# The first block's attention: the value products of two query tiles in one group, 256 columns wide

## The chip, the cores and the metric

The kernel runs on one core of one Trainium2 chip. The metric is the device time of one execution in microseconds (us). The kernel before took 1542.6 us, the median of 3 runs (1541.73 to 1544.58). In names of engines, PE is TensorE, ACT ScalarE, DVE VectorE, POOL GpSimd and SP SyncE.

## The reference, cut to what matters

Two blocks, each of two layers, work on 256 tokens of width 1024. The change is in the attention of the first block. Its layer 0 also updates a stream of 256 context tokens, its layer 1 does not.

```python
def first_block(...):
    for l in range(DEPTH):                       # DEPTH = 2
        ...
        o = jnp.concatenate([
            global_attention(qa, ka, va, kac, vac),            # 6 heads, 256 + 256 keys
            fourier_mix(fb),
            window_attention(qc, kc, vc, kcc, vcc, sink[l]),   # 6 heads, 256 + 256 keys, window and sink
        ], axis=-1)
        x = x + gt1 * (o @ w_out[l])
        ...
        if update_ctx:                           # layer 0 only
            oc = jnp.concatenate([
                dense_attention(qac, kac, vac),                # 6 heads, 256 keys
                fourier_mix(fbc),
                dense_attention(qcc, kcc, vcc, sink[l]),
            ], axis=-1)
            ...
```

Each attention is softmax(q k^T / 8) times v, for heads of 64 channels. Everything is in 32-bit floats.

## The kernel before, in words

Five engines run one program each, tied by semaphores that count finished work. The order on each engine is written out by hand in loops; nothing reorders it later.

**Steps and pairs.** `pairs_first` makes a list of attention steps. One step is one pair of heads and one tile of 128 queries (`u["n"]` is 0 or 1). Steps 2p and 2p+1 are the two query tiles of the same two heads: pair p. Layer 0 has 12 steps of the x stream against 512 keys (w = 512) and then 12 of the context stream against 256 keys (w = 256). Layer 1 has only the 12 of w = 512. From the seventh step of each stream on, a head has a sink, and in the x stream a window mask.

**One step** goes through these operations:

- `logits` (L1097, PE): scores of both heads into two PSUM banks.
- `shifts` (DVE): the mask is added (L2209), the row maximum taken (L2210) and turned into a shift (L2212, or L2215 and L2217 with a sink).
- `probs` (L1537, ACT): the exponential, with its row sum.
- `shares` (L2226 and L2230, DVE): division by the sum.
- `turn_probs` (L1117, PE): transposes of the probabilities, by 128 columns, into the two banks `TURN`; a step of w = 512 fills both, a step of w = 256 fills one.
- `keep_turned` (L1552, ACT): copies these banks to `probT` in SBUF. There are two places for `probT`, and a step uses the one of its number modulo 2, so step j overwrites what step j-2 left. That is why ACT first waits until the value products of step j-2 are done: `act.wait_ge(pv_done, u["step"] - 1)`. The next step's transposes wait in turn for these copies, since they need the banks.
- `values` (L1130, PE): the value products. For each of the w/128 chunks of keys and each of two heads, one product with 64 value channels as weights and the 128 turned query columns as moving data. The two heads write the upper and the lower 64 partitions of bank `OUT`, and the two steps of a pair its columns 0 to 127 and 128 to 255.
- `empty_out` (L1576, ACT): after the second step of a pair, bank `OUT` goes to `mixo`. `lead` (L1566, ACT) rounds it into the operand of the output projection, and POOL (L2735) keeps the rest.

**The order.** On PE, loop turn i issues `logits(i)`, `turn_probs(i-3)`, a piece of other work where `BESIDE_AT` has 2i, `values(i-4)`, and another piece where it has 2i+1. The other work is the modulation vectors (`ada_sums` L838, `ada_spread` L853 and L857, `ada_spread_ctx` L864; all use bank `BESIDE`) and the Fourier mixing (L1169, then L1174 and L1175). On ACT, turn i issues `keep_turned(i-3)`, `empty_out(i-4)`, `probs(i)`, in some turns the copies of the Fourier products (L1612, L1625), `lead(i-4)`, and in two turns of each layer the rounding of a weight unit for the output projection (`split_ahead`, L1428, 2048 columns): i = 11 and 14 in layer 0, i = 5 and 7 in layer 1. On DVE, turn i issues `shifts(i)`, a piece of the other work, `shares(i-1)` and another piece (L1905, L1908 and L1913 for the modulation vectors, L2285 for the Fourier mixing, L1887 for a weight unit's remainder).

Bank `OUT` is free for a new pair once `empty_out` of the pair before is done. The output projection (L823 to L825) follows on PE right behind the last value product.

## Time and profile before

| | us |
|---|---|
| median of 3 runs (range) | 1542.6 (1541.73 to 1544.58) |
| the profiled execution, its time | 1544.52 |
| its span | 1542.7 |
| the attention of layer 0 in it | 107.8 to 200.9 |
| the attention of layer 1 in it | 692.8 to 744.9 |

The span is what the profiler saw of one execution, from the first instruction to the last; the execution's own time is 1.8 us more. Times of the trace count from the start of the span. PE's busy time holds matmuls whose records overlap, since they are pipelined, so what a block of them costs is the distance from its first start to the next block's start. The trace has two records for each matmul of plain 32-bit floats: a program's eight stand as x16. Transposes have one each.

### The profile page before, as it was taken

How to read it: one execution, taken by the hardware profiler on the slowest of the kernel's cores; microseconds unless marked ns; L12 is line 12 of the kernel's file. 1: busy time of each engine (PE TensorE's matmuls, PEld its weight loads, DVE VectorE, ACT ScalarE, POOL GpSimd, SP SyncE). 2: the span in 40 equal slices, each digit the busy share in tenths (PEclk: the TensorE clock that was granted, in tenths of full speed). 3: DMA queues.
4: the chain of work that ended last, by engine and by line, in shares of the span. 5: the costliest groups of instructions: out<-in, count | busy, mean ns of one | idle time of the engine just before them, and what ended most of it. 6: DMA issues, size and time to landing. Idle time of an engine off the chain costs nothing.

```text
span 1542.7 us, 23297 instructions
## 1 busy us (share of the span) xinstructions
PE 1494.9 (97%) x9195; PEld 1254.5 (81%) x9195; DVE 1076.0 (70%) x1613; ACT 680.0 (44%) x1073; POOL 144.8 (9%) x151
## 2 busy tenths in 40 slices
PE   6999999999999999999999999899999999999998
PEld 3775579888888888885789999788988988898896
DVE  2748645778887886758466667688766777876566
ACT  3446725221121212538453333655555656455463
POOL 1210102000000000410100000321000111200002
PEclk9999999999999999999999999999999999999999
DMA  9526423454445633235345555645533555463342
GB/s 335 198 96 214 101 76 116 156 178 144 148 160 210 239 118 108 84 109 137 110 135 185 179 184 164 199 155 178 172 94 126 162 160 170 151 198 111 125 141 90
DMA packets 169422, 235.86 MB, mean 153 GB/s; under 512 B 9020, under 2 KB 116580, under 8 KB 169192
## 3 DMA queue, kind: packets, MB, share of 16 engines
q1 hardware_dynamic: 169320, 234.45, 46.7%
q8 instruction: 70, 1.15, 0.3%
q14 instruction: 32, 0.26, 0.1%
HBM read 233.38 MB, written 1.05 MB: 152 GB/s over the span
## 4 chain that ended last, share of the span: by engine, by line
PE 85%; DVE 7%; ACT 3%; issue 2%; POOL 1%; DMA 1%; SPq 0%; POOLq 0%; DVEq 0%; ACTq 0%
PE psum L823 24%; PE psum L825 23%; PE psum L824 23%; PE psum L1097 3%; PE psum L1130 3%; PE psum L1117 3%; DVE wl L1887 2%; PE psum L838 1%; PE psum L1025 1%; PE psum L957 1%; PE psum L1169 1%; ACT wh L1428 1%; DVE smax L2210 1%; DMA raw<-in_w_ada 1%; ACT hTh L1662 1%
## 5 line engine op out<-in xcount | busy, mean ns | idle before, releaser
L1887 DVE TENSOR_TENSOR wl<-raw,wh 128x2048 fp32r<-128x2048 f32 (+1 forms) x170 | 384.8, 2263 | 165.7 <-ACT wh L1428 99.0
L823 PE MATMUL psum<-hTh,wh 128*128 128x256 f32 (+1 forms) x1376 | 430.0, 313 | 5.1 <-DVE hTl L2010 3.5
L825 PE MATMUL psum<-hTh,wl 128*128 128x256 f32 (+1 forms) x1376 | 423.1, 307 | 0.0
L824 PE MATMUL psum<-hTl,wh 128*128 128x256 f32 (+1 forms) x1376 | 423.1, 307 | 0.0
L1777 ACT ACTIVATE wh<-raw 128x2048 fp32r<-128x2048 f32 x62 | 118.9, 1918 | 371.6 <-PE psum L825 371.6
L823 PEld LDWEIGHTS psum<-hTh,wh 128*128 128x128 f32 x1376 | 262.3, 191 | 23.5 <-issue 6.9
L824 PEld LDWEIGHTS psum<-hTl,wh 128*128 128x128 f32 x1376 | 262.4, 191 | 13.4 <-issue 0.7
L825 PEld LDWEIGHTS psum<-hTh,wl 128*128 128x128 f32 x1376 | 262.3, 191 | 12.6
L1428 ACT ACTIVATE wh<-raw 128x2048 fp32r<-128x2048 f32 (+2 forms) x108 | 202.4, 1874 | 108.7 <-PE psum L825 97.1
L823 PE MATMUL psum<-wh,hTh 128*128 128x512 f32 (+3 forms) x576 | 222.1, 386 | 9.3 <-DVE hTl L1989 4.0
L825 PE MATMUL psum<-wh,hTl 128*128 128x512 f32 (+3 forms) x576 | 218.0, 378 | 0.0
L824 PE MATMUL psum<-wl,hTh 128*128 128x512 f32 (+3 forms) x576 | 217.6, 378 | 0.0
L823 PEld LDWEIGHTS psum<-wh,hTh 128*128 128x128 f32 x576 | 109.0, 189 | 33.9 <-issue 8.7
L825 PEld LDWEIGHTS psum<-wh,hTl 128*128 128x128 f32 x576 | 109.0, 189 | 18.8
L824 PEld LDWEIGHTS psum<-wl,hTh 128*128 128x128 f32 x576 | 109.2, 190 | 17.3
L823 PE MATMUL psum<-wh,ffh 128*128 128x512 f32 x264 | 104.9, 397 | 0.1
L825 PE MATMUL psum<-wh,ffl 128*128 128x512 f32 x264 | 102.9, 390 | 0.0
L824 PE MATMUL psum<-wl,ffh 128*128 128x512 f32 x264 | 102.9, 390 | 0.0
L2210 DVE TENSOR_REDUCE smax<-psum 128x2 f32<-128x1024 f32 (+3 forms) x68 | 61.9, 910 | 54.4 <-PE psum L1097 31.5
L2366 DVE TENSOR_TENSOR scr<-psum,scr 128x512 f32<-128x512 f32 x108 | 70.5, 687 | 19.0 <-PE psum L825 18.7
L1552 ACT ACTIVATE work<-psum 128x512 f32<-128x512 f32 (+1 forms) x104 | 55.1, 565 | 41.0 <-PE psum L1117 40.9
L1537 ACT ACTIVATE work<-psum,shift 128x256 f32<-128x256 f32 (+4 forms) x118 | 64.5, 556 | 19.1 <-DVE shift L2212 16.6
(207 smaller groups left out, 1805.5 us busy)
## 6 DMA issues: line engine op xcount, KB each, us to landing
raw<-in_w_in SPq DMA_DIRECT2D x54, 1024.0 KB, 5.0
raw<-in_w_ada SPq DMA_DIRECT2D x24, 1024.0 KB, 5.2
raw<-in_w_gate SPq DMA_DIRECT2D x22, 1024.0 KB, 5.1
raw<-in_w_up SPq DMA_DIRECT2D x22, 1024.0 KB, 5.2
raw<-in_w_down SPq DMA_DIRECT2D x22, 1024.0 KB, 4.8
qkT<-in_w_ada SPq DMA_DIRECT2D x16, 1024.0 KB, 7.2
raw<-in_w_in SPq DMA_DIRECT2D x16, 768.0 KB, 4.5
vals<-in_w_ada SPq DMA_DIRECT2D x8, 1024.0 KB, 6.4
```

Source lines behind the costliest of these rows:

```text
L823: pe.matmul(o, left[0], right[0], start=first, stop=False)
L824: pe.matmul(o, left[0], right[1], start=False, stop=False)
L825: return pe.matmul(o, left[1], right[0], start=False, stop=last)
L1097: mm = pe.matmul(o[:, x, g * nk:g * nk + nk], u["q"][g][x], u["k"][g][x], start=g * nk % 512 == 0, stop=True, skip_group_check=True)
L1117: mm = pe.transpose(o[:, P * x:P * x + P], u["score"][:, f:f + P], ident[:, :])
L1428: act.activation(wh[:, w % SPLIT, 0:m], raw[:, u % RING, 0:m], ACT.Copy).then_inc(hi_ready, 1)
L1537: act.activation(u["score"][:, x * u["w"]:x * u["w"] + u["w"]], u["logits"][:, x, :], ACT.Exp, bias=shift[:, s, x:x + 1], scale=SCALE, acc ...
L1552: act.activation(flat[:, 512 * n:512 * n + m], ps[TURN[(u["turn0"] + n) % 2]][:, 0:m], ACT.Copy)\
L1777: act.activation(wh[:, w % SPLIT, :], raw[:, u % RING, :], ACT.Copy).then_inc(hi_ready, 1)
L1887: dve.tensor_tensor(wl[:, w % SPLIT, 0:m], raw[:, u % RING, 0:m], wh[:, w % SPLIT, 0:m].bitcast(F32), ALU.subtract).then_inc(lo_ready, 1)
L2210: link(dve.tensor_reduce(smax[:, s, :], u["logits"], AX.X, ALU.max))
L2366: dve.tensor_tensor(y, ps[down_bank(l, i, x)], y, ALU.add).then_inc(ysum_done, 1)
```

## The change

In the first block only, `values` does nothing in the first step of a pair. In the second step it makes the products of both query tiles: the two places of `probT` are read as one operand of 2 x 128 columns (`both`), so each product has 256 columns. There are eight of them for a pair of w = 512 and four for w = 256, where there were sixteen and eight. `pv_done` still rises by two for a pair, once at the last product of each head. For the first step of a pair, ACT's wait in `keep_turned` is raised by one: the copy into place 0 now waits for the whole pair before, whose products read it. The bank is asked for in the second step alone. Everything else is unchanged, `empty_out` among it, and the second block's attention too.

```diff
                 def values(u):
 
+                    if not second and u["n"] == 0:
+                        return
                     pe.wait_ge(probT_ready, u["turn1"])
                     at = OUT
+                    if not second:
+                        bank(at)
+                        n = u["w"] // P
+                        both = work[:, 3072:5120].rearrange("p (t c q) -> p t c q", t=2, q=P)
+                        for c_ in range(n):
+                            for x in range(2):
+                                mm = pe.matmul(ps[at][HD * x:HD * x + HD, 0:SEQ].rearrange("p (t q) -> p t q", t=2),
+                                               u["vs"][x][c_], both[:, :, n * x + c_, :], start=c_ == 0,
+                                               stop=c_ == n - 1, skip_group_check=True)
+                                if (c_, x) == (n - 1, 0):
+                                    mm.then_inc(pv_done, 1)
+                        mm.then_inc(pv_done, 1)
+                        freed[at] = (out_emptied, u["pair"] + 1)
+                        return
                     if u["n"] == 0:
                         bank(at)
...
                     u = steps[j]
                     if j >= 2:
-                        act.wait_ge(pv_done, u["step"] - 1)
+                        act.wait_ge(pv_done, u["step"] - 1 + (not second and u["n"] == 0))
```

PE in layer 0, from the value products of step 0 (the rows between the sums and spreads of the modulation vectors), before:

```order
L853 MATMUL psum<-adar,sel 128x512
L1130 MATMUL psum<-work,vals 64x128 x8
L864 MATMUL psum<-adar,sel 128x512
L1097 MATMUL psum<-qkT 128x512 x2
L1117 MATMUL psum<-ident,work 128x128 x8
L1130 MATMUL psum<-work,vals 64x128 x8
L838 MATMUL psum<-raw,csil 32x512 x8
```

and the same place in the changed kernel, where the value products are L1133:

```order
L853 MATMUL psum<-adar,sel 128x512
L864 MATMUL psum<-adar,sel 128x512
L1097 MATMUL psum<-qkT 128x512 x2
L1117 MATMUL psum<-ident,work 128x128 x8
L1133 MATMUL psum<-work,vals 64x256 x8
L838 MATMUL psum<-raw,csil 32x512 x8
```

The first block of value products is gone from between the two spreads, and the second is twice as wide.

PE at the end of layer 1's attention, from the transposes of step 8 to the output projection, before:

```order
L1117 MATMUL psum<-ident,work 128x128 x8
L1174 MATMUL psum<-four,dftC 128x256
L1175 MATMUL psum<-four,dftC 128x256
L1130 MATMUL psum<-work,vals 64x128 x8
L1117 MATMUL psum<-ident,work 128x128 x8
L1130 MATMUL psum<-work,vals 64x128 x8
L1169 MATMUL psum<-dftL,vals 128x512 x2
L1117 MATMUL psum<-ident,work 128x128 x8
L1130 MATMUL psum<-work,vals 64x128 x8
L1117 MATMUL psum<-ident,scr 128x128 x8
L1174 MATMUL psum<-four,dftC 128x256
L1175 MATMUL psum<-four,dftC 128x256
```

and in the changed kernel:

```order
L1117 MATMUL psum<-ident,work 128x128 x8
L1190 MATMUL psum<-four,dftC 128x256
L1191 MATMUL psum<-four,dftC 128x256
L1133 MATMUL psum<-work,vals 64x256 x8
L1117 MATMUL psum<-ident,work 128x128 x8
L1185 MATMUL psum<-dftL,vals 128x512 x2
L1117 MATMUL psum<-ident,work 128x128 x8
L1133 MATMUL psum<-work,vals 64x256 x8
L1117 MATMUL psum<-ident,scr 128x128 x8
L1190 MATMUL psum<-four,dftC 128x256
L1191 MATMUL psum<-four,dftC 128x256
```

The transposes of steps 9 and 11 now stand directly behind the wide products of pairs 3 and 4, or with the Fourier products alone between them; the value products of steps 8 and 10 are gone from there.

## Rows read from the trace of the kernel before

**Rows 1.** The page's part 1: busy time, share and instructions of each engine.

```profile
PE 1494.9 (97%) x9195; PEld 1254.5 (81%) x9195; DVE 1076.0 (70%) x1613; ACT 680.0 (44%) x1073; POOL 144.8 (9%) x151
```

**Rows 2.** Busy time by stretch (start:end, length, then engines, PE clock, DMA, GB/s).

```profile
107.80:200.90 93.10, 89.43 (x681) 49.44 (x680) 66.25 (x175) 64.45 (x178) 8.02 (x11) 0.98 0.50 148
692.80:744.90 52.10, 48.80 (x390) 28.06 (x389) 39.92 (x86) 39.89 (x96) 3.64 (x5) 1.00 0.41 102
```

**Rows 3.** Waits of PE in layer 0's attention: total, times, longest, us.

```profile
PE psum L1117 <- ACT work L1552: 2.1, 1, 2.1
PE psum L1169 <- DVE hTl L2285: 1.0, 1, 1.0
...
```

**Rows 4.** Waits of PE in layer 1's attention.

```profile
PE psum L1117 <- ACT work L1552: 1.8, 2, 1.5
PE psum L1169 <- DVE hTl L2285: 0.6, 1, 0.6
PE psum L1130 <- ACT work L1552: 0.4, 1, 0.4
PE psum L1097 <- ACT sunk L1541: 0.4, 1, 0.4
```

**Rows 5.** Timeline of PE, layer 0 (start, length, what, [idle before <-releaser]).

```profile
126.33 1.09 PE L1130 MATMUL psum<-work,vals 128*64 128x128 f32 x16
127.36 1.92 PE L838 MATMUL psum<-raw,csil 128*32 128x512 f32 x16
129.21 1.13 PE L1097 MATMUL psum<-qkT 64*128 64x512 f32 x4
130.27 1.09 PE L1117 MATMUL psum<-ident,scr 128*128 128x128 f32 x8
...
182.70 0.70 PE L1097 MATMUL psum<-qkT 64*128 64x256 f32 x4
183.33 0.66 PE L1117 MATMUL psum<-ident,work 128*128 128x128 f32 x4
183.92 0.66 PE L1130 MATMUL psum<-work,vals 128*64 128x128 f32 x8
184.50 0.70 PE L1097 MATMUL psum<-qkT 64*128 64x256 f32 x4
```

**Rows 6.** Timeline of layer 0 behind the value products of step 0: PE, then DVE.

```profile
123.19 1.13 PE L864 MATMUL psum<-adar,sel 128*128 128x512 f32 x2
...
122.46 0.69 DVE L1913 COPY gates<-psum 128x512 f32<-128x512 f32 x1
```

**Rows 7.** Timeline of ACT, layer 0, its turn 11.

```profile
158.39 1.91 ACT L1428 ACTIVATE wh<-raw 128x2048 fp32r<-128x2048 f32 x1 [0.69 <-DMA raw<-in_w_out]
```

**Rows 8.** Timeline of layer 1, turns 5 and 6: PE, then ACT.

```profile
714.72 1.06 PE L1117 MATMUL psum<-ident,work 128*128 128x128 f32 x8 [0.34 <-ACT work L1552]
...
708.89 1.08 ACT L1552 ACTIVATE work<-psum 128x512 f32<-128x512 f32 x2
710.26 0.38 ACT L1576 ACTIVATE mixo<-psum 128x256 f32<-128x256 f32 x1 [0.29 <-PE psum L1130]
...
713.97 1.09 ACT L1552 ACTIVATE work<-psum 128x512 f32<-128x512 f32 x2
716.35 1.12 ACT L1552 ACTIVATE work<-psum 128x512 f32<-128x512 f32 x2
...
718.62 0.69 ACT L1537 ACTIVATE scr<-psum,shift 128x512 f32<-128x512 f32 x1 [0.88 <-DVE sunk L2217]
```

**Rows 9.** Timeline of layer 1, its end: PE, then ACT.

```profile
733.91 1.09 PE L1117 MATMUL psum<-ident,work 128*128 128x128 f32 x8
...
743.87 1.09 PE L1130 MATMUL psum<-work,vals 128*64 128x128 f32 x16 [0.43 <-ACT work L1552]
744.89 0.50 PE L823 MATMUL psum<-wh,hTh 128*128 128x512 f32 x1
...
734.02 0.38 ACT L1576 ACTIVATE mixo<-psum 128x256 f32<-128x256 f32 x1 [1.19 <-PE psum L1130]
```

## The prediction

> **What bounds the kernel now.** I read the page's busy times first: PE is busy for 97% of the span [rows 1]. The change touches two stretches only, so I read those next. In both, PE keeps its full clock (0.98 and 1.00) and is busy for 89.4 of 93.1 us in layer 0's attention and 48.8 of 52.1 us in layer 1's; ACT is busy for 64.5 and 39.9 us [rows 2]. Two things follow. Time that a block of PE's work costs there is nearly always on the path. But the stretches are also the narrowest place for the other engines: DVE and ACT are at 70 to 77%, and each step is a ring PE, DVE, ACT, DVE, PE, ACT, PE. The waits show how near that ring is to binding: PE waits 3.1 us or so for others in layer 0 [rows 3] and 3.2 us in layer 1, three of the four kinds for ACT [rows 4]. So the change has to be read twice: as work on PE, and as new moments at which ACT may start.
>
> **Part 1: work on PE.** A block's cost is the distance between starts [rows 5]. A value block of w = 512 costs 127.36 - 126.33 = 1.03 us, one of w = 256 costs 184.50 - 183.92 = 0.58. The difference, 0.44 us, is four products of 128 columns, so a block has 1.025 - 2 x 0.44 = 0.15 us that doesn't depend on its length. The wide block is not in this trace. The nearest rows for "same matmuls, twice the columns" are the scores: 183.33 - 182.70 = 0.63 for 256 columns and 130.27 - 129.21 = 1.06 for 512, so 256 more columns of a two-head pair cost 0.43 us, in full proportion. Four such pairs and the fixed 0.15 make 1.855 us for a wide block, 1.0 for the context stream's. Bounds: 1.71 if only the columns count (four times 0.43) and nothing is fixed, and 2.05 if nothing is saved against two blocks. I take 1.855. Saved per pair: 2 x 1.025 - 1.855 = 0.20 and 2 x 0.585 - 1.0 = 0.17 us. In layer 0 that is 6 x 0.20 + 6 x 0.17 = 2.2 us, in layer 1 6 x 0.20 = 1.2 us.
>
> The Trainium skill, in "TensorE: Matmul & The Clock Gate", section "Back-to-back issue gap", gives 81 ns per matmul at 128 columns and 131 ns at 512 in a sustained stream; an estimate on a straight line between them is 98 ns at 256, so 1.57 us for the sixteen records of a wide block, 1.7 with the fixed part. The trace's sixteen records of 128 columns take 64 ns each and its scores grow in proportion, so I don't follow it. By it the sum below would be 2.2 us smaller.
>
> **Part 2: what was hidden behind the first steps' blocks.** Several removed blocks stood where PE would have waited anyway. In layer 0, the block of step 0 lies between the two spreads, and the second spread can't start before DVE has copied bank `BESIDE` (122.46 + 0.69 = 123.15; the spread starts at 123.19) [rows 6]. Without the block PE idles for 1.03 us there: nothing is gained, and the pair's work comes later on top.
>
> **Part 3: the new wait on ACT.** The first copy of every pair but the first now starts when the wide block of the pair before has ended. PE issues that block in the same turn, behind the transposes: where ACT could copy step j's transposes while PE made the products of step j-1, it now stands still for 1.86 us, plus any piece between. Behind this wait on ACT are the copies (two, 0.97 us apart from start to next start), `empty_out`, the exponentials (1.4 us), `lead` and the rounding of a weight unit (1.8 us). For ACT wait, in turn: the next step's transposes (they need both banks), the scores two steps on (exponentials free their banks), and DVE.
>
> I walked both stretches with these durations, PE, ACT and DVE side by side, each operation starting at the later of its predecessor's end and its inputs plus 0.04 us. With the order of before, the walk gives the last value block's start at 744.4 us (743.87 in the trace, [rows 9]), so it may be used for differences.
>
> *Layer 1, against before:*
>
> - Turn 5. Step 0's block is gone (-1.02), pair 0's is wide (+0.83): it ends at 710.0. ACT's copy of step 2 moves from 708.89 to 710.1 [rows 8]. ACT had 0.29 us of slack in front of `empty_out` [rows 8] and loses the rest: +0.77 on everything behind it, the rounding included. PE's transposes of step 4, which waited for ACT at 714.72 already [rows 8], come 0.77 late, whatever PE saved.
> - Turn 7. Pair 1's wide block adds 0.83, so PE is 1.6 late at its end. The copy of step 4 stands at 718.5 instead of 716.35 [rows 8]; 0.88 us of idle time before the exponentials [rows 8] takes up some of it. ACT is +1.1, with the second rounding behind it, and so are the transposes of step 6.
> - Turns 9 to 11. Pair 2 adds 0.83 (+1.9), step 6's block gives back 1.02 (+0.9), pair 3 adds 0.83 (+1.7). The transposes of step 9 come directly behind it [rows 9]; the copy of step 8 can start only then, and its first half takes 0.6: PE waits 0.7 (+2.5). ACT's exponentials of step 11 are late by as much, with them the Fourier copies: +2.7 at the next Fourier product, though step 8's block is gone.
> - The end. Pair 4 adds 0.83 and the transposes of step 11 wait 0.7 for the copy of step 10 (+4.3); step 10's block is gone, but the last block waits for its copies anyway, 1.6 us where it waited 0.43 [rows 9]; it is 0.83 longer. Layer 1: **+5.1 us**, which is -1.2 of work and +6.3 of waits.
>
> *Layer 0:* it has more work beside, which covers the copies. It adds 1.03 us at the second spread; 0.9 at the last L857, which was covered by step 6's block while DVE copied; 0.2 and 1.1 in turns 12 and 13, where no piece stands beside: the copy of step 8 and so the exponentials of step 11 are 2 us late. The rounding at 158.39 waited for its transfer [rows 7] and now waits for ACT until 159.9, so the 2.1 us wait of the transposes [rows 3] moves by +1.4 rather than shrinking. At the end, 1.1 and 0.6 more at the last Fourier product and the last block. Together 4.9 of waits (rounded), less 2.2 of work: **+2.6 us**.
>
> Behind layer 1's stretch the projection starts right at the last block's end on PE [rows 9], behind layer 0's too, and its weights are fetched as units are used up, so the whole rest moves by as much. Sum: **+7.7 us**. The profiled execution took 1544.5 us and would take 1552.2; it lay 1.9 above the median, so the median goes from 1542.6 to **1550.3 us**. With a wide block of 1.71 us the same walk gives +5.6, with 2.05 +11.1 (1548.2 and 1553.7).
>
> **The rivals.**
>
> 1. *PE alone counts* (faster). If the waits are swallowed, because ACT has 30.8% of the stretch idle in layer 0 and PE is the bound, only the work counts: -2.2 - 1.2 = -3.4 us, 1539.2 us. That ACT idles speaks for it; that its idle time lies in front of the transposes while the new wait lies behind them speaks against. It decides where PE has over 1.2 us of other work between the wide block and the transposes that need the copy; in layer 1 that is so behind pair 2 alone. The Trainium skill, in "Perfetto Trace Analysis", section "Identifying the Most-Contended Engine", says to optimize the busiest engine first, which is PE here, and so leans to this rival.
> 2. *The new wait costs nothing, the shift of the work does.* If ACT gets through its copies in time, what is left is Part 2 and the later, longer last block: 3.4 us of waits less 2.2 in layer 0, 3.3 less 1.2 in layer 1, +3.3 us: 1545.9 us.
> 3. *No change that can be measured.* The gain of rival 1 in layer 0 against a loss in layer 1, or a stretch behind that takes up the delay: near 1543 us. Against it, the output projection follows the last block without a gap: 743.87 + 1.02 is the start of L823 at 744.89 [rows 9].
> 4. *The ring locks.* Each wide block waits for copies that wait for the wide block before, in the context stream too, where scores and transposes are only 0.63 and 0.58 us. With 0.6 us more for each of its six pairs: +11.5 us, 1554 us.
>
> **Chances.** A measurement of this kernel can tell about 0.2% (3.1 us) from no change. My forecast with its bounds of block cost has 0.66, rival 1 0.05, rival 2 0.12 (on the edge of that bound), rival 3 0.07, rival 4 0.10. Slower: the forecast, rival 4 and most of rival 2, 0.87; same 0.08; faster 0.05. The range runs from 1545.8, which takes in rival 2, to 1553.8, the dear block.
>
> **What the profile would show.** Right: value blocks x16 with a distance of 1.8 to 1.9 us; the first copy of each pair waiting for the value products, by far the largest wait of ACT in both stretches; PE's wait for ACT's copies in layer 1 up from 1.8 to some 5 us; the last value block of layer 1 ending 7 to 8 us later than before, 5 of them within that stretch. Wrong: wide blocks much under 1.8 us, or transposes behind a wide block that don't wait; then rival 2 or 1 holds. A gap that isn't PE's wait for ACT or DVE would be something I haven't seen.

## The result and the profile after

| | before | after |
|---|---|---|
| median of the runs made together, us | 1542.97 (1541.73 to 1544.58, 4 runs) | 1560.88 (1559.56 to 1561.65, 4 runs) |
| the profiled execution, its time | 1544.52 | 1560.91 |
| its span | 1542.7 | 1559.1 |

The changed kernel takes 1.0115 times as long (95% interval 1.0097 to 1.0132), 17.9 us more. The forecast was 7.7 more. (One execution of the kernel before in the third comparison below, 2960.21 us, was disturbed and is left out everywhere.)

Part 1 of the profile's page for the changed kernel, which answers to [rows 1]:

```profile
PE 1499.2 (96%) x8955; PEld 1248.3 (80%) x8955; DVE 1078.0 (69%) x1613; ACT 679.0 (44%) x1073; POOL 144.4 (9%) x151
```

PE has 240 records less and is busy for 4.3 us *more*. Work that was taken away can't do that. The busy time by stretch says where to look; these are the same two stretches as in [rows 2], from the first scores to the first matmul of the output projection, with the same columns:

```profile
108.90:207.26 98.36, 89.32 (x538) 43.99 (x537) 67.72 (x175) 63.42 (x178) 8.03 (x11) 0.97 0.47 140
699.00:761.17 62.17, 52.41 (x294) 26.89 (x293) 41.56 (x86) 39.86 (x96) 3.65 (x5) 0.92 0.34 85
```

| part of the span, us | before | after | difference |
|---|---|---|---|
| start to layer 0's attention | 107.8 | 108.9 | +1.1 |
| layer 0's attention | 93.2 | 98.4 | +5.1 |
| between | 491.7 | 491.7 | 0 |
| layer 1's attention | 52.15 | 62.17 | +10.0 |
| the rest | 797.8 | 797.9 | +0.1 |

(Starts and ends of both kernels are taken at the same instructions, the first scores and the first matmul of the output projection; so layer 0 before is 93.2 here and 93.1 in [rows 2].) The loss is in the two stretches that the change touches; the first line differs between executions whatever the kernel (106.3 to 108.9 in the profiles of this study). In layer 1, PE's busy time rose from 48.8 to 52.4 us although 96 records went, and PE's granted clock, the third number from a row's end, fell from 1.00 to 0.92.

The waits of PE in layer 0's attention, and then in layer 1's, after (total, times, longest, us):

```profile
PE psum L1117 <- ACT work L1568: 2.6, 2, 2.4
PE psum L1185 <- DVE hTl L2301: 2.1, 1, 2.1
PE psum L864 <- DVE gates L1929: 1.3, 1, 1.3
PE psum L1097 <- ACT sunk L1557: 1.1, 1, 1.1
PE psum L1133 <- ACT work L1568: 1.0, 1, 1.0
PE psum L857 <- DVE adar L1924: 0.9, 1, 0.9
```

```profile
PE psum L1117 <- ACT work L1568: 4.6, 4, 1.5
PE psum L1185 <- DVE hTl L2301: 1.8, 1, 1.8
PE psum L1133 <- ACT work L1568: 1.5, 1, 1.5
PE psum L1097 <- ACT sunk L1557: 0.9, 1, 0.9
PE psum L1097 <- ACT work L1553: 0.8, 1, 0.8
```

These are the waits that the walk had forecast. In layer 0 they sum to 9.0 us, in layer 1 to 9.6, against 3.5 and 3.2 before. (The prediction said 3.1 for layer 0: the list of [rows 3] goes on with 0.4 us of the value products' wait for ACT's copy.) Most of them come from ACT, whose copies of the transposes (L1568) now wait for the wide value products (L1133). The waits of ACT after, first layer 0, then layer 1:

```profile
ACT work L1568 <- PE psum L1133: 21.4, 8, 4.4
```

```profile
ACT work L1568 <- PE psum L1133: 11.0, 5, 2.8
```

So the mechanism is the forecast one, but it accounts for 6.4 us more of waiting in layer 1 and for 1.0 us less of work. The stretch grew by 10.0, so 4.6 us are missing. They stand in PE's timeline of layer 1 (start, length, what, idle before):

```profile
713.40 1.09 PE L1117 MATMUL psum<-ident,work 128*128 128x128 f32 x8
714.42 1.95 PE L1133 MATMUL psum<-work,vals 128*64 128x256 f32 x16
716.30 1.13 PE L1097 MATMUL psum<-qkT 64*128 64x512 f32 x4
...
719.29 1.13 PE L1097 MATMUL psum<-qkT 64*128 64x512 f32 x4 [0.83 <-ACT work L1553]
721.88 1.94 PE L1117 MATMUL psum<-ident,work 128*128 128x128 f32 x8 [1.46 <-ACT work L1568]
723.75 2.42 PE L1133 MATMUL psum<-work,vals 128*64 128x256 f32 x16
726.10 1.13 PE L1097 MATMUL psum<-qkT 64*128 64x512 f32 x4
...
731.77 1.94 PE L1117 MATMUL psum<-ident,work 128*128 128x128 f32 x8 [1.46 <-ACT work L1568]
733.64 2.60 PE L1133 MATMUL psum<-work,vals 128*64 128x256 f32 x16
736.17 1.98 PE L1185 MATMUL psum<-dftL,vals 128*128 128x512 f32 x4
...
748.71 3.63 PE L1185 MATMUL psum<-dftL,vals 128*128 128x512 f32 x4 [1.77 <-DVE hTl L2301]
752.18 1.04 PE L1117 MATMUL psum<-ident,work 128*128 128x128 f32 x8
...
759.29 1.95 PE L1133 MATMUL psum<-work,vals 128*64 128x256 f32 x16 [1.45 <-ACT work L1568]
761.17 0.50 PE L823 MATMUL psum<-wh,hTh 128*128 128x512 f32 x1
```

Read the same block twice. The wide products take 716.30 - 714.42 = 1.88 us, and 726.10 - 723.75 = 2.35 or 736.17 - 733.64 = 2.53 where the transposes just ahead of them had waited. Eight transposes take 1.02 us (714.42 - 713.40) at the first of these rows and 1.87 (723.75 - 721.88) behind a wait, and the Fourier product takes 3.47 at 748.71 and 1.91 to 1.98 elsewhere. Each time a wait of PE lies just ahead. The granted clock of those three places (busy time by stretch again, the clock third from the end):

```profile
721.88:726.10 4.22, 4.22 (x24) 2.82 (x25) 4.05 (x8) 1.77 (x6) 0.00 (x0) 0.66 0.18 59
731.77:736.17 4.40, 4.40 (x25) 2.89 (x25) 2.19 (x7) 1.78 (x6) 0.00 (x0) 0.63 0.00 0
748.71:752.18 3.47, 3.47 (x5) 1.40 (x6) 2.78 (x8) 0.77 (x2) 0.60 (x1) 0.52 0.00 0
```

PE waited, and then ran for a while at 1.2 GHz, half of its full 2.4. One such fall costs 1.7 us. The three rows lose 4.22 x 0.34 = 1.4, 4.40 x 0.37 = 1.6 and 3.47 x 0.48 = 1.7, and the first two are cut at the blocks' ends; a stretch that holds the whole first fall, 718 to 730 us, has the clock at 0.86 and so loses 12.0 x 0.14 = 1.7. Layer 0 has two falls after. One is at the last Fourier product, behind a wait of 2.1 us. The other follows the wait of 2.4 us, but the transposes right behind that wait took 1.06 us, nearly their usual time; the wide block after them, 3.45 us from its start to the next block's, is the slow one:

```profile
165.15 3.52 PE L1133 MATMUL psum<-work,vals 128*64 128x256 f32 x16
```

Before had one too, and I had not seen it. Its clock in two stretches of layer 0, and the blocks there:

```profile
162.00:163.50 1.50, 1.50 (x17) 1.17 (x17) 1.46 (x4) 1.16 (x4) 0.00 (x0) 0.63 1.00 205
163.50:166.50 3.00, 3.00 (x5) 1.12 (x4) 0.61 (x2) 1.60 (x6) 0.73 (x1) 0.62 1.07 245
```

```profile
161.93 1.58 PE L1130 MATMUL psum<-work,vals 128*64 128x128 f32 x16
163.44 3.14 PE L1169 MATMUL psum<-dftL,vals 128*128 128x512 f32 x4
```

A value block of 1.51 us instead of the 1.03 of [rows 5]: the 0.98 of [rows 2] is this one fall, 1.7 of 93.1 us. The same profile has three more outside the two stretches, near 26, 771 and 971 us, behind waits of PE of 3.3, 2.4 and 1.9 us. It also has, in layer 1, a wait of 1.46 us ahead of the transposes with no fall behind it:

```profile
722.90 1.06 PE L1117 MATMUL psum<-ident,work 128*128 128x128 f32 x8 [1.46 <-ACT work L1552]
```

### The profile page after: what moved, and what is told of

Read it like the earlier page. It is cut to its first block, busy times and chain, and to the rows that moved or that the text cites. A ratio compares the mean times of both kernels' runs of the same rounds, so it can differ in the third digit from the quotient of the medians.

```text
span 1559.1 us, 22818 instructions
## 1 busy us (share of the span) xinstructions
PE 1499.2 (96%) x8955; PEld 1248.3 (80%) x8955; DVE 1078.0 (69%) x1613; ACT 679.0 (44%) x1073; POOL 144.4 (9%) x151
## 4 chain that ended last, share of the span: by engine, by line
PE 85%; DVE 7%; ACT 3%; issue 2%; POOL 1%; DMA 1%; SPq 0%; POOLq 0%; DVEq 0%; ACTq 0%
PE psum L823 24%; PE psum L825 23%; PE psum L824 23%; PE psum L1097 3%; PE psum L1117 3%; DVE wl L1903 2%; PE psum L1133 2%; PE psum L1146 1%; PE psum L957 1%; PE psum L838 1%; PE psum L1025 1%; PE psum L1185 1%; DVE smax L2226 1%; ACT wh L1444 1%; DMA raw<-in_w_ada 1%
## 5 line engine op out<-in xcount | busy, mean ns | idle before, releaser
L823 PEld LDWEIGHTS psum<-wh,hTh 128*128 128x128 f32 x576 | 108.9, 189 | 34.2 <-issue 9.0
L1568 ACT ACTIVATE work<-psum 128x512 f32<-128x512 f32 (+1 forms) x104 | 55.3, 567 | 62.7 <-PE psum L1133 32.4
```

The source lines that it names most:

```text
L823: pe.matmul(o, left[0], right[0], start=first, stop=False)
L1568: act.activation(flat[:, 512 * n:512 * n + m], ps[TURN[(u["turn0"] + n) % 2]][:, 0:m], ACT.Copy)\
```

## The experiments

Two theories stood at first: the waits alone, with PE at its usual rate (what was forecast), or waits plus the clock that falls behind them. A third question was whether the width of the products is worth anything by itself.

Numbers of a job are held against the kernel before in the same job. Its medians were 1542.8 (10 runs), 1542.92 (7) and 1542.9 (20) in the three jobs. Each run also lists its mean granted clock over the span. What the clock took from a run is then about (1 - clock) x 1541 us, and I give the median with that taken off as "without the clock's loss". For before it is 1536.9, 1537.3 and 1537.1, for the change 1546.6 in the first comparison. It is an estimate. A thousandth of clock, to which the clocks are given, is 1.5 us; single runs of the changed kernel scatter from 1544.1 to 1548.1 in it, so I don't read differences under 1 us. And it takes every fall at its whole 1.7 us, those outside the two stretches too, where that isn't shown: behind layer 1 the profiles have 797.8 us with two falls (before) and 797.2 with one (`e8_before_ahead`).

### Layer 0 alone, layer 1 alone

Each step's own flag takes the place of the change's condition. `e1_only_layer0`, and the same with `(1,)` for `e2_only_layer1`:

```diff
                 u["step"], u["turn0"], u["pair"] = att_at["step"], att_at["turn"], att_at["pair"]
+                u["late"] = step == "att1" and l in (0,)
...
-                    if not second and u["n"] == 0:
+                    if u["late"] and u["n"] == 0:
                         return
...
-                    if not second:
+                    if u["late"]:
...
-                        act.wait_ge(pv_done, u["step"] - 1 + (not second and u["n"] == 0))
+                        act.wait_ge(pv_done, u["step"] - 1 + (u["late"] and u["n"] == 0))
```

> The change in layer 0's attention alone; layer 1 as before. Theory A (new waits in the rings of both layers, made dearer by TensorE's clock, which the records of the changed kernel show at 0.50 to 0.56 behind the longer waits): layer 0's stretch takes 98.4 us as in the changed kernel (93.2 before), layer 1's 52.2 as before, and the time is 5 to 6 us over the kernel before. Theory B (part of the loss is something outside the two stretches, such as the start): the excess over before is more than 7 us.

> The change in layer 1's attention alone; layer 0 as before. Theory A: layer 1's stretch takes 62.2 us (52.2 before), layer 0's 93.2, and the time is 10 to 11 us over the kernel before; with the other run the two excesses add up to the whole change's 17.9 within 2 us. Theory B: they add up to clearly less, and a part of some 3 us belongs to neither stretch.

Measured: layer 0 alone 1549.82 us (1547.07 to 1551.82), ratio 1.0049 (1.0032 to 1.0066); layer 1 alone 1551.28 (1549.48 to 1552.53), ratio 1.005 (1.0033 to 1.0067). Over the 1542.8 of before that is 7.0 and 8.5 us, together 15.5. The expectations were missed in their sizes: layer 0 alone cost more than the 5 to 6 us expected, layer 1 alone less than 10 to 11, and the sum misses the first comparison's 17.9 by 2.4 where at most 2 were expected; the change itself came to 14.4 and 14.9 in the later jobs. Without the clock's loss they are 1540.9 and 1543.3: +4.0 and +6.4, together 10.4, where the whole change has 9.3 to 9.7. The busy time by stretch of `e1_only_layer0`'s layer 0:

```profile
107.58:203.60 96.02, 87.48 (x537) 43.63 (x536) 67.65 (x175) 63.23 (x178) 8.01 (x11) 0.98 0.49 143
```

and of `e2_only_layer1`, its untouched layer 0, then its layer 1:

```profile
107.85:199.13 91.28, 87.91 (x681) 48.62 (x680) 66.32 (x175) 64.46 (x178) 8.02 (x11) 1.00 0.51 151
690.83:751.78 60.95, 51.34 (x294) 25.96 (x293) 41.45 (x86) 39.86 (x96) 3.66 (x5) 0.94 0.36 87
```

The second row is worth more than it looks. It is the *unchanged* layer 0, with the same 681 records of PE as [rows 2], in 91.28 instead of 93.2 us: in this execution the fall at 162 us didn't happen. The wait ahead of that place was a little shorter too, 1.8 us instead of 2.1, so this alone doesn't show that a fall is a matter of the execution; `e5_after_again` below does. Layer 1 has two falls here where the change's profile had three, and is 1.2 us shorter. The losses of the layers add up, and each has a part that is no clock.

### A third place for the transposed probabilities

`e3_third_place` removes what makes ACT wait. There are three places of 1024 columns: the first steps of pairs take turns between two of them and the second steps keep the third, so the first copy of a pair goes to one that the pair before doesn't use. The scores that used the new place's columns go elsewhere.

```diff
-                held = scr[:, 0, :] if step == "att1" and i % 4 == 3 else work[:, at:at + 1024 + 512 * (u["kind"] == "M")]
+                if step == "att1" and i % 4 == 2:
+                    at_t = 2048
+                held = qkT[:, 5120:6144] if step == "att1" and i % 4 == 2 else scr[:, 0, :] if step == "att1" and i % 4 == 3 else work[:, at:at + 1024 + 512 * (u["kind"] == "M")]
...
-                        both = work[:, 3072:5120].rearrange("p (t c q) -> p t c q", t=2, q=P)
+                        both = work[:, 2048:5120].rearrange("p (t c q) -> p t c q", t=3, q=P)
+                        both = both[:, 0:3:2] if u["pair"] % 2 else both[:, 1:3]
...
-                    if j >= 2:
-                        act.wait_ge(pv_done, u["step"] - 1 + (not second and u["n"] == 0))
+                    if j >= 2 and (second or u["n"]):
+                        act.wait_ge(pv_done, u["step"] - 1)
+                    elif j >= 4:
+                        act.wait_ge(pv_done, u["step"] - 2)
```

> The changed kernel, where the turned probabilities of first steps alternate between two places, so that ACT's first copy of a pair no longer needs the pair before it to be multiplied, but the one before that (one score buffer is moved to free it). The wide products and their place in PE's order stay. Theory A (ACT's new wait is the cause): ACT's wait for value products before its copies, 21.4 and 11.0 us in the changed kernel, is gone, and with it more than half of the loss: layer 1's stretch takes 54 to 56 us instead of 62.2, layer 0's 94 to 96 instead of 98.4, the time 3 to 6 us over the kernel before (the later place of the products alone costs 3.3 by my walk). Theory C (the late place of the wide products and the covers they took away are the cause, not ACT's wait): both stretches stay within 1 us of the changed kernel.

Measured: 1547.6 us (1546.96 to 1548.14, 7 runs), ratio 1.0029 (1.0018 to 1.0041); without the clock's loss 1540.8. Busy time by stretch, and all of the copies' waits that are left, layer 0 and layer 1 (here L1573 is the copy and L1119 the transposes):

```profile
107.76:202.55 94.79, 87.59 (x538) 43.38 (x537) 67.14 (x175) 64.15 (x178) 8.01 (x11) 0.98 0.48 145
694.27:748.75 54.48, 47.82 (x294) 24.26 (x293) 40.62 (x86) 40.01 (x96) 3.65 (x5) 1.00 0.40 97
```

```profile
ACT work L1573 <- PE psum L1119: 8.3, 8, 2.4
```

```profile
ACT work L1573 <- PE psum L1119: 1.0, 1, 1.0
```

No copy waits for the value products any more (21.4 and 11.0 us did), layer 1's stretch is 54.48 at full clock, and 10 to 13 us of the kernel's time (1557.3 to 1560.9 for the change, in other jobs, 1547.6 here) are gone. The new wait of ACT's copies is therefore the cause of most of the loss, clock and all. Part of it has only moved: ACT now waits for the wide products one operation later, in `empty_out`, 11.5 us in layer 0 and 5.3 in layer 1, where it waited 4.8 and 1.8 before. Of the 4.8 us that stay over before, I took the cause to be the later value blocks at both ends of each stretch; `e11_hybrid` below shows that they are less than half of it. PE computes less in `e3_third_place` than before and the kernel is still slower.

### Idle matmuls in the waits

If the clock falls because PE stands still, then work in the gap should keep it, even useless work. `e4_filled` puts matmuls of `ident` by `ident` into a free bank, in layer 1, six ahead of the transposes that wait in turns 7 and 9 and eight in turn 12. `e9_filled_both` adds nine at each of two places of layer 0.

```diff
+FILL = {7: (1, 6), 9: (3, 6)}
...
+                    if not second and len(steps) == 12 and i in FILL:
+                        pe.wait_ge(out_emptied, steps[FILL[i][0]]["pair"] + 1)
+                        for _ in range(FILL[i][1]):
+                            pe.matmul(ps[OUT][:, 0:P], ident[:, :], ident[:, :], start=True, stop=True,
+                                      skip_group_check=True)
+                    if not second and len(steps) == 24 and i == 13:
+                        o = bank(BESIDE)
+                        for _ in range(9):
+                            pe.matmul(o[:, 0:P], ident[:, :], ident[:, :], start=True, stop=True,
+                                      skip_group_check=True)
                     if 0 <= i - lag < len(steps):
                         turn_probs(steps[i - lag])
...
```

(Not shown: the same loops for turn 12 of layer 1 and turn 24 of layer 0, into bank `OUT`.)

> The changed kernel with idle matmuls (128 columns, 32-bit, into bank OUT, which is empty there; their result is overwritten) in three places of layer 1's attention where PE waits anyway: six before the transposes of step 4, six before those of step 6 (1.3 us each, in waits of 1.46), and eight before the Fourier product that waits 1.77. Theory A (the clock falls behind these waits, and blocks at half the clock cost 4.4 us in layer 1): the blocks behind (transposes 1.87 us, wide blocks 2.35 and 2.53, Fourier product 3.47) take their full-clock 1.02, 1.88, 1.88 and 1.91, the stretch takes 57.5 to 59.5 us instead of 62.2, and the time falls by 3 to 4.5 us against the changed kernel, though PE does more. Theory D (these blocks are long for another reason, such as what they wait for while they run): the stretch stays at 62 us or grows.

> The changed kernel once more, unaltered, on the chip of the next three kernels. In its first profile layer 0's stretch took 98.4 us, but 96.3 in the profile of the kernel with idle matmuls, whose layer 0 is the same code; and the part ahead of the attention took 1.1 us more than elsewhere. Theory A1 (whether a wait lets the clock fall is a matter of how the execution happens to lie, so medians of runs move by 2 us and more from job to job): the median lies somewhere from 1555 to 1561 us and layer 0's stretch at 96 to 98.4. Theory A2 (it is a property of the program): 1559.5 to 1562 and 98.4 again.

> The changed kernel with idle matmuls in both layers: the three places of layer 1 as in the earlier filled kernel, and in layer 0 nine before the transposes of step 10 (into the free bank BESIDE, in a wait of 2.4 us) and nine before the last Fourier product (into bank OUT, in a wait of 2.15). Theory A (9 us of waits in the rings, and on top 1.7 us for each wait behind which the clock falls): 1551 to 1553 us, a mean granted clock of 0.996 or more as in the kernel before, no stretch at half the clock in the profile, layer 0 at 94.5 to 95, layer 1 at 57.1 to 57.7; the changed kernel beside it in this job at 1556 to 1561 with a clock of 0.990 to 0.994. Theory D (the clock is no cause but goes with slow executions): the same time as the changed kernel in this job.

> The changed kernel unaltered, beside the kernels with idle matmuls in this job: 1556 to 1561 us, clock 0.990 to 0.994; the time less the span times (1 minus the mean clock) about 9 us over the same of the kernel before, as in both jobs so far.

`e5_after_again` and `e12_after_third` are the changed kernel, unaltered, in the second and third job. Measured:

| | job | median (range), us | ratio (95%) | mean clock | without the clock's loss |
|---|---|---|---|---|---|
| `e4_filled` | 1 | 1552.77 (1551.98 to 1555.92) | 1.007 (1.0053 to 1.0087) | 0.9955 | 1546.4 |
| `e5_after_again` | 2 | 1557.33 (1556.51 to 1559.87) | 1.0099 (1.0082 to 1.0115) | 0.9930 | 1546.9 |
| `e9_filled_both` | 3 | 1551.87 (1550.37 to 1552.12) | 1.0056 (1.0041 to 1.007) | 0.9968 | 1546.4 |
| `e12_after_third` | 3 | 1557.82 (1557.04 to 1560.39) | 1.0099 (1.0085 to 1.0114) | 0.9920 | 1546.4 |

`e4_filled` alone settled nothing. No changed kernel ran beside it, and in its profile layer 1 took 57.66 us with no fall, but the unfilled one of `e5_after_again` took 57.67, with none either:

```profile
698.00:755.67 57.67, 48.05 (x293) 24.27 (x292) 41.46 (x86) 39.92 (x96) 3.64 (x5) 1.00 0.38 92
```

```profile
720.89 1.06 PE L1117 MATMUL psum<-ident,work 128*128 128x128 f32 x8 [1.46 <-ACT work L1568]
721.88 1.95 PE L1133 MATMUL psum<-work,vals 128*64 128x256 f32 x16
...
744.84 1.98 PE L1185 MATMUL psum<-dftL,vals 128*128 128x512 f32 x4 [1.77 <-DVE hTl L2301]
```

The wait of 1.46 us is the same as at 721.88 above, to the hundredth, and the transposes behind it take 1.0 us, not 1.87. So the wait alone doesn't decide it: the same program, with the same wait, has the fall in one execution and not in another. The third profile of the same kernel has the falls again. `e9_filled_both`, then `e12_after_third`, layer 1, one job:

```profile
693.72:751.36 57.64, 52.74 (x333) 28.95 (x332) 41.46 (x86) 39.87 (x96) 3.63 (x5) 1.00 0.36 92
```

```profile
695.15:757.73 62.58, 52.90 (x293) 26.90 (x293) 41.56 (x86) 39.83 (x96) 3.63 (x5) 0.92 0.34 85
```

`e9_filled_both` executes 40 records more on PE in that stretch and is 4.9 us shorter there. Its median is 6.0 us under that of the unfilled kernel in the same job, while the figure without the clock's loss is the same, 1546.4. The fillers add next to nothing to the path and give back what the clock took. That is the test that tells the theories apart: with the waits alone, matmuls in them could gain nothing. It also gives the size: the change costs 1546.4 - 1537.1 = 9.3 us that don't depend on the clock, and 5 to 8.5 us in clock.

One expectation was missed: layer 0 of `e9_filled_both` took 95.66 us without a fall, not 94.5 to 95. Two things made it longer. The nine matmuls ahead of the last Fourier product overfill their wait by 0.3 us. And the rounding of the weight unit waited 0.75 us for its transfer, where it waited for none in the profile of `e12_after_third`, so that PE's transposes of step 10 came later.

### The same filler in the kernel before

`e10_before_filled` puts the nine matmuls at i = 13 into the kernel before, ahead of its transposes that wait for 2.1 us [rows 3].

> The kernel before with nine idle matmuls ahead of the transposes of step 10 in layer 0, where it waits 2.1 us and the profile then shows half the clock for 3.4 us, in which 1.7 us are lost. Theory A: no stretch at half the clock in the attention, layer 0's stretch at 91.3 to 91.7 instead of 93.2 where it had fallen, the time 0 to 1.7 us under the kernel before (its runs don't all have the fall), the mean clock up from 0.9965 to 0.997 or 0.998. Theory D: no change.

Measured: 1542.65 us (1541.57 to 1543.79, 11 runs) against 1542.9, ratio 0.9997 (0.9988 to 1.0006): no change that can be measured. Its layer 0, and the blocks at the place of the fall:

```profile
107.70:199.38 91.68, 90.09 (x699) 50.70 (x698) 66.34 (x175) 64.46 (x178) 8.01 (x11) 1.00 0.50 150
```

```profile
158.69 2.27 PE L1143 MATMUL psum<-ident 128*128 128x128 f32 x18
...
162.97 1.98 PE L1174 MATMUL psum<-dftL,vals 128*128 128x512 f32 x4
```

The fall is gone from this profile (the Fourier product takes 1.98 us, not 3.14), but over eleven runs the filler brings hardly anything back: the mean clocks are 0.9967 and 0.9961, which is 0.9 us, half a fall a run. Part of even that goes to the filler itself. It takes 2.26 us (160.95 - 158.69), where PE was idle for 1.8 us in one profile (`e2_only_layer1`) and 2.1 in another. The fall of before's profile isn't in all of its runs, and a profile's one execution must not be taken for all.

### The order of products and transposes

In the change PE issues a wide block behind the transposes of the next step. `e6_values_ahead` issues it ahead of them, so that ACT's copy needn't wait for it, and `e8_before_ahead` does the same to the kernel before, as a control.

```diff
+                    if i == lag + 1:
+                        pe.wait_ge(evac_act, vals_ready)
+                    if not second and 0 <= i - lag - 1 < len(steps):
+                        values(steps[i - lag - 1])
                     if 0 <= i - lag < len(steps):
                         turn_probs(steps[i - lag])
                     next(beside, None)
-                    if i == lag + 1:
-                        pe.wait_ge(evac_act, vals_ready)
-                    if 0 <= i - lag - 1 < len(steps):
+                    if second and 0 <= i - lag - 1 < len(steps):
                         values(steps[i - lag - 1])
```

> The changed kernel with the wide products ahead of the step's transposes on PE instead of behind them, so ACT's first copy of a pair finds the pair before multiplied when its own transposes land. Theory A (ACT's wait is most of it): ACT's wait for value products before its copies goes, layer 1's stretch takes 54 to 57 us, layer 0's 95 to 98, the time is 4 to 9 us over the kernel before; the value products themselves now wait for the copies of the step before (about 2 us in two turns of layer 1, by my walk), since a rounding of a weight unit stands in front of them on ACT. Theory C (place of the wide products): no better than the changed kernel, 1558 us or more.

> The kernel before with its narrow products ahead of the transposes, as a control for the order alone. By my walk layer 0's stretch loses 5 us and layer 1's 2.3, since the products of every step now stand where their copies are not yet made; with the clock on top 1548 to 1555 us. If the order alone costs that, it explains what the kernel with the wide products ahead keeps of the loss; if it costs under 2 us, the order is free and what remains there is the width's.

Measured: 1553.65 us (1552.5 to 1554.88), ratio 1.0072 (1.0055 to 1.0089), and for the control 1550.26 (1549.74 to 1550.89), ratio 1.0046 (1.0029 to 1.0063). The first is 10.7 us over before where 4 to 9 were expected, a miss. The waits of PE for ACT move from the transposes to the value products. Layer 0, first `e6_values_ahead`, then `e8_before_ahead` (`mixo` is `empty_out`'s):

```profile
PE psum L1133 <- ACT work L1570: 4.2, 6, 2.3
```

```profile
PE psum L1130 <- ACT work L1554: 2.8, 3, 1.7
PE psum L1130 <- ACT mixo L1578: 2.3, 4, 1.1
```

The order costs the kernel before 7.3 us by itself, since the products need the copy that has just been made and the transposes then stand behind their wait. With the change on top it is 3.4 us more, where the change in its own order costs 14.4 in that job. Those 3.4 us go with the clock (mean 0.9935 against 0.9970); without falls the two stretches together take 151.0 us in `e6_values_ahead` (96.73 less one fall, and 55.93) and 151.3 in `e8_before_ahead` (96.37 and 54.92), so in this order the change costs and gains hardly anything beyond it, though it takes 3 us of work off PE. So the wide block's harm is in where it stands in ACT's way, but this order is no cure.

### Is it the width or the place?

`e7_narrow_moved` keeps the block in the second step and all its waits, but makes two products of 128 columns for each wide one, `pv_done` rising after the first query tile's and at the end.

```diff
-                        for c_ in range(n):
-                            for x in range(2):
-                                mm = pe.matmul(ps[at][HD * x:HD * x + HD, 0:SEQ].rearrange("p (t q) -> p t q", t=2),
-                                               u["vs"][x][c_], both[:, :, n * x + c_, :], start=c_ == 0,
+                        for t in range(2):
+                            for c_ in range(n):
+                                for x in range(2):
+                                    mm = pe.matmul(ps[at][HD * x:HD * x + HD, P * t:P * t + P],
+                                                   u["vs"][x][c_], both[:, t, n * x + c_, :], start=c_ == 0,
...
```

> The change's place and waits with the old width: both query tiles' products of a pair in the second step, but as two sets of 128 columns. What the width alone saves is a block's distance: I expect 2.0 us for the double block against 1.88 for the wide one, and with it 2 to 4 us over the changed kernel, measured beside it in this job (eighteen pairs by 0.1 to 0.17, nearly all on the path). If the width mattered otherwise (or not at all), the two are equal.

Measured: 1557.9 us (1554.85 to 1559.35), ratio 1.01 (1.0083 to 1.0117); without the clock's loss 1545.4. That is equal to the changed kernel beside it (1557.33), where I had expected it to be 2 to 4 us slower: a miss. (Without the clock's loss it is even 1.5 us lower than the changed kernel's 1546.9, at the edge of what that figure can tell.) The timeline says why:

```profile
730.05 1.97 PE L1134 MATMUL psum<-work,vals 128*64 128x128 f32 x32
731.95 1.98 PE L1186 MATMUL psum<-dftL,vals 128*128 128x512 f32 x4
```

32 records of 128 columns take 731.95 - 730.05 = 1.90 us, 16 of 256 take 1.88. The width saves 0.02 us a block. What Part 1 of the prediction counted as saved (0.17 to 0.20 a pair) is real, but it comes from having one block where there were two: 2 x 1.025 - 1.90 = 0.15 us, which a block has whatever its length.

### Can any of it be kept?

`e11_hybrid` takes the third place of `e3_third_place`, leaves the first and the last pair of each stretch as before, and has the filler at i = 13.

```diff
+                u["late"] = step == "att1" and 2 <= i < len(steps) - 2
```

> Wide products where they may pay: the third place for turned probabilities, the first and the last pair of each attention in narrow products at their old places, the idle matmuls of layer 0 before step 10's transposes. By the walk this gives back the 1.0 us at the second spread and 2 us at the end of each stretch: layer 0 at 91 to 92, layer 1 at 52.2 to 53, the time within 2 us of the kernel before. If width could pay in this ring, this is where it would show as less than 1542; if more than 1545, the place in the middle costs by itself.

Measured: 1544.54 us (1543.77 to 1545.99, 11 runs), ratio 1.0011 (1.0002 to 1.002); without the clock's loss 1539.6, 2.5 over before. Its stretches take 91.93 and 53.81 us, without a fall, against the 91.28 and 52.15 that before's take without one. Of the loss nearly all is gone and none of a gain has come: 1.6 us over before. That is within the 3.1 us that I called no change, but the interval excludes 1, so it is a small loss. Layer 1 missed the 52.2 to 53 us expected. Against `e3_third_place` 3.1 us are gone. By the mean clocks (0.9953, 0.9965) 1.8 of them are clock; without the clock's loss the step is from +3.9 to +2.5, and this 1.4 is what the first and last pairs' later blocks cost (up to 1.8, as the filler can cost 0.4 itself). The 2.5 that stay belong to the pairs in the middle; their cause was not tested. In layer 1 PE still waits 2.8 us for ACT's copies at the transposes (1.8 before) and 1.6 for DVE at the Fourier product (0.6 before). The width brings nothing to set against what is left, and no version here beats the kernel before.

## Why the prediction was wrong in its size

**The direction and the mechanism held.** Part by part:

- *Part 1, work on PE.* Forecast 1.855 us for a wide block, measured 1.88, so 0.17 saved a pair instead of 0.20. The lower price of 1.71, and with it the estimate from the Trainium skill, don't hold. The reason that I gave, a fixed 0.15 us per block, is what `e7_narrow_moved` showed.
- *Part 2, the block behind the first spread.* Forecast 1.03 us of waiting at L864; the profile has 1.3.
- *Part 3, the new wait.* The walk forecast the transposes of step 4 0.77 late; they start 22.88 us into the stretch (721.88 - 699.00) instead of 21.98 (714.72 - 692.74), +0.90. It forecast about 5 us of PE's waits for ACT's copies at the transposes of layer 1, and the profile has 4.6; 1.6 us at the last block, and it has 1.5. ACT's wait for the value products is its largest, as said. The stretch of layer 1 without falls is 57.67 us in `e5_after_again`, +5.5 where +5.1 was forecast; that of layer 0 is 98.36 - 2 x 1.7 = 95.0 in the first profile and 94.3 in two others (96.02 and 95.95, less one fall), against 91.3 to 91.5 before, +2.8 to +3.7 where +2.6 was. Together 8.3 to 9.2 and, by the runs' clocks, 9.3 to 9.7, for 7.7 forecast. In layer 0 the walk had 4.9 us of new waits and the profile's rose by 5.5, from 3.5 to 9.0. The largest part of that difference is a step that I had put at nothing: the rounding of the weight unit, I said, "now waits for ACT" and no longer for its transfer. It did wait for its transfer, 0.39 us in this profile and 0.49 in `e5_after_again`, and PE's transposes of step 10 waited 2.4 and 2.5 us; in `e12_after_third` and `e1_only_layer0` it didn't, and they waited 1.9.
- *Behind the stretches* nothing moved: 491.7 and 797.9 us, as forecast.

**The step that failed** is the sentence that opens the reading: "In both, PE keeps its full clock (0.98 and 1.00)". 0.98 is not full. It was one fall of 1.7 us, behind the very wait [rows 3] that the prediction spoke of, and all durations of the sum were those of full clock. Had I looked at the clock in short stretches there, I would have priced a long wait of PE at its own length plus, at times, 1.7 us, and the change had five falls in the stretches of its first profile. Of the measured 17.9 us some 9.3 to 9.7 don't depend on the clock and the rest does: (0.9960 - 0.9905) x 1541 = 8.5, with the mean clock of before from the first job's ten runs, since the first comparison lists only its profiled execution (0.995). In the two others it was 5.1 and 6.3 by the same sum (0.9963 - 0.9930, 0.9961 - 0.9920), and the whole loss 14.4 and 14.9. The forecast of 7.7 would have been low by 1 to 2 us even at an even clock.

The Trainium skill has this in "TensorE: Matmul & The Clock Gate", whose section "The HAM clock gate (the "warmup" mystery)" says that the clock is throttled by default and that activity releases it, and that the same kernel differs from run to run since the monitor's periods run free of it. The rows agree with both: the falls lie behind waits, and one wait of 1.46 us has a fall behind it in two profiles of the changed kernel and none in the third. I had taken a figure for a block from that page and not its first subject.

**The rivals.** Rival 1 (PE alone counts, -3.4 us) is out: the work it counted as saved was saved, and the waits took it back fourfold (3.1 us by 18 pairs of 0.17, against 9.3 + 3.1 without the clock). Rival 2 (+3.3) is out by the waits of ACT. Rival 3 is out: the interval, 1.0097 to 1.0132, excludes it. Rival 4 gave +11.5, the nearest time, for the wrong reason: it had every pair of the context stream wait, and the profile has the transposes of layer 0 wait for ACT's copies twice in all, 2.6 us.

**What stays open.** Why one and the same wait lets the clock fall in one execution and not in the next was not settled; the profiles show only that it does. Waits of other lengths were not tried for it. In layer 1 each wait of 1.46 us has another close ahead of it (0.8 and 0.9 us in the changed kernel, 0.4 before); whether that matters was not tried either. And the medians of the change in three comparisons (1560.88, 1557.33, 1557.82) differ by 3.5 us, in step with their clocks (0.9905, 0.9930, 0.9920), for a reason that I can't name.

## What to carry to other kernels

Where two blocks of matmuls become one, ask first which engine waits for the earlier of the two: a buffer that both now hold to the end turns a copy that ran beside them into a link of the ring, and here 3 us saved on PE came with 12 us more of waits. Read the granted clock in stretches as short as a block, before anything is priced: 0.98 over 93 us was a fall worth half of the smallest change that could be measured, and every new wait of PE may bring another. To tell a wait from its clock, put useless matmuls into it, no longer than the wait, and compare medians; (1 - mean clock) x span taken off each run is an estimate of the same. The profile of one execution doesn't tell.

## What the runs showed of the hardware

- A fall of TensorE's clock from 2.4 to 1.2 GHz cost 1.7 us each time, in the two stretches behind waits of PE of 1.46, 1.77, 2.1 and 2.4 us, elsewhere in the kernel before behind 1.9, 2.4 and 3.3. The same waits of 1.46 and 1.77 us had none behind them in `e5_after_again`.
- PE got slower by being idle: with twenty useless matmuls in layer 1's waits (333 records for 293) and eighteen in layer 0's, the median fell from 1557.82 to 1551.87 us in one job. Layer 1's stretch took 57.64 us for 62.58.
- A fall need not start in the block right behind the wait: behind the wait of 2.4 us the transposes took 1.06 us (1.0 at the full clock) and the wide block after them 3.45 instead of 1.88.
- Medians of one kernel that differ by 3.5 us agree within 0.5 once (1 - clock) x 1541 us is taken off each run: 1546.6, 1546.9, 1546.4 for the change in three comparisons, 1546.4 with the fillers in two jobs. Single runs scatter more (1544.1 to 1548.1).
- Products of 128 and of 256 columns cost the same by the column (1.90 and 1.88 us for one block's worth). A block costs 0.15 us more whatever its length: 0.58, 1.03 and 1.90 us for 8, 16 and 32 records of 128 columns.
